# Moving the latent norm behind a whole projection job, and a weight split behind the key rotation, in a hand-scheduled transformer kernel

## The reference

```python
h = _rmsnorm(x, norm_g[l])
p = _split(h @ w_in[l])               # all projections of the layer
# branch A: latent attention
q  = _rmsnorm(cq, qa_g) @ w_uq        # cq: 256 features, its own norm
kv = _rmsnorm(ckv, kva_g) @ w_ukv     # ckv: 128 features, its own norm
k_rope = _rope(krope, cos, sin)       # a rotated key of 32 features
# branch C: sparse attention
score = relu(einsum('bqhd,bkd->bqhk', qidx, kidx))
index = einsum('bqh,bqhk->bqk', widx, score) * idx_scale
_, sel = lax.top_k(index, 128)        # 128 keys for each query
# branch B: differential attention; branch D: a gated short convolution
x = x + y @ w_out[l]
```

## Time and profile before

| what | value |
|---|---|
| median of 3 runs | 1886.48 us (1883.54 to 1887.06) |
| the profiled execution, its own time | 1886.48 us |
| span of the profiled execution | 1884.7 us |
| mean granted clock of PE | 0.992 |
| busy: PE | 1850.3 us, 98% |
| busy: PEld, DVE, ACT, POOL | 78%, 55%, 37%, 20% |
| chain that ended last, by engine | PE 93%, DVE 3%, issue 2%, ACT 1%, DMA 1% |

### The profile page before, as it was taken

The page is one execution under the profiler, slowest core; times in us unless marked ns, Lnnn a source line. Parts: engine busy times, 40 slices in busy tenths (PEclk is TensorE's granted clock), DMA queues, the critical chain, the costliest instruction groups (busy, mean ns, idle before and its releaser), DMA issues.

```text
span 1884.7 us, 26241 instructions
## 1 busy us (share of the span) xinstructions
PE 1850.3 (98%) x9284; PEld 1466.1 (78%) x9284; DVE 1038.5 (55%) x2106; ACT 691.8 (37%) x1274; POOL 386.1 (20%) x223
## 2 busy tenths in 40 slices
PE   6999999999999999999999999999999999999998
PEld 4767777876777788888888777778887888888887
DVE  5789777578977755554433333333644654454332
ACT  3444444335444432332233343333323423233222
POOL 2435253433534330000000222220110200000000
PEclk9999999999999999999999999999999999999999
DMA  5222112222211233222333412222221222232332
GB/s 190 76 82 68 57 56 81 91 68 79 77 58 53 84 123 95 100 94 95 101 107 105 140 56 68 81 77 79 90 90 45 79 90 90 100 100 90 105 107 89
DMA packets 48577, 165.65 MB, mean 88 GB/s; under 512 B 5592, under 2 KB 6104, under 8 KB 48472
## 3 DMA queue, kind: packets, MB, share of 16 engines
q1 hardware_dynamic: 47176, 161.88, 26.2%
q10 hardware_dynamic: 1296, 2.42, 0.4%
HBM read 162.12 MB, written 2.17 MB: 87 GB/s over the span
## 4 chain that ended last, share of the span: by engine, by line
PE 93%; DVE 3%; issue 2%; ACT 1%; DMA 1%; POOL 0%; POOLq 0%; DVEq 0%; SPq 0%; ACTq 0%
PE proj L863 75%; PE score L1081 3%; PE o L1117 2%; PE turned L1093 2%; PE proj L1236 2%; PE proj L1240 1%; PE turned L1304 1%; PE score L1298 1%; PE o L1328 1%; PE turned L833 1%; DVE wlo L1794 1%; PE o L1392 1%; PE score L1381 1%; ACT whi L1440 1%; PE proj L995 1%
## 5 line engine op out<-in xcount | busy, mean ns | idle before, releaser
L863 PE MATMUL proj<-hhi,whi 128*128 128x512 f32 x1488 | 600.2, 403 | 4.0 <-DVE wlo L1794 2.1
L863 PE MATMUL proj<-hlo,whi 128*128 128x512 f32 x1488 | 582.7, 392 | 0.0
L863 PE MATMUL proj<-hhi,wlo 128*128 128x512 f32 x1488 | 582.7, 392 | 0.0
L1440 ACT ACTIVATE whi<-ring 128x1024 fp32r<-128x1024 f32 x266 | 281.4, 1058 | 698.8 <-PE proj L863 652.8
L863 PEld LDWEIGHTS proj<-hhi,whi 128*128 128x128 f32 x1488 | 281.2, 189 | 97.6 <-issue 34.0
L863 PEld LDWEIGHTS proj<-hhi,wlo 128*128 128x128 f32 x1488 | 281.0, 189 | 60.8
L863 PEld LDWEIGHTS proj<-hlo,whi 128*128 128x128 f32 x1488 | 281.6, 189 | 55.9 <-issue 1.0
L1794 DVE TENSOR_TENSOR wlo<-ring,whi 128x1024 fp32r<-128x1024 f32 x187 | 228.5, 1222 | 158.8 <-ACT whi L1440 158.7
L655 POOL TENSOR_TENSOR wlo<-ring,whi 128x1024 fp32r<-128x1024 f32 x79 | 189.8, 2402 | 445.1 <-ACT whi L1440 445.0
L668 POOL TENSOR_TENSOR prob<-prob 128x512 f32<-128x512 f32 x30 | 46.3, 1544 | 854.6 <-ACT prob L1436 854.2
L1466 ACT ACTIVATE prob<-prob,negmax 128x256 f32<-128x256 f32 (+3 forms) x208 | 114.4, 551 | 136.0 <-DVE negmax L1838 136.0
(11 more groups left out here) (219 smaller groups left out, 2209.7 us busy)
## 6 DMA issues: line engine op xcount, KB each, us to landing
ring<-wstream SPq DMA_DIRECT2D x288, 512.0 KB, 3.5
arena<-lines SPq DMA_DIRECT2D x28, 256.0 KB, 5.5
arena<-x ACTq DMA_DIRECT2D x4, 512.0 KB, 6.2
out<-arena SPq DMA_DIRECT2D x8, 256.0 KB, 2.9
arena<-mem SPq DMA_DIRECT2D x1, 1024.0 KB, 9.4
par<-params ACTq DMA_DIRECT2D x3, 74.0 KB, 1.9
arena<-hot SPq DMA_DIRECT2D x2, 85.0 KB
arena<-rope SPq DMA_DIRECT2D x1, 128.0 KB, 6.0
```

Of the source, the lines that this page charges most:

```text
L863: mm = pe.matmul(b, rounded(w), rounded(rhs(v, k)), start=(first and n == 0 and p == 0), stop=(last and n == len(blocks) - 1 and p == 2))
L1440: act.activation(rounded(dst), src, ACT.Copy, scale=scale).then_inc(ready, 1)
```

## The change

- Sums of the latent squares: `LATENT_AT` goes from chunks 5 and 7 of BQ0 and 1 of BK0 to chunks 1, 3 and 5 of BK0.
- PE's wait for the diagonals and the 16 spreading matmuls go from behind chunk 0 of VT0 to behind the whole of VT0.
- DVE takes the means behind the eviction of BK0 instead of behind half 0 of the top-k; the diagonals come behind three small operations on `lam`, and no longer between half 2 and the eviction of BK0.
- `TOPK_EARLY` goes from 5 to 7: four halves (3 to 6) lie between the diagonals and the attention steps. They and the eviction of VT0 now stand ahead of the scaling of the latent tiles, not behind it.
- POOL takes the root behind the low part made after BK0 (the slot of BQ1), not ahead of it.
- POOL multiplies for the key rotation ahead of the low part made after KR (the slot of CQ1), not behind it, and ACT copies ahead of the high part of that slot.

```diff
-LATENT_AT = ((2, 5), (2, 7), (3, 1))
+LATENT_AT = ((3, 1), (3, 3), (3, 5))
...
-TOPK_FIRST, TOPK_EARLY = 3, 5
+TOPK_FIRST, TOPK_EARLY = 3, 7
...
 # POOL
                 prepare_after("KI")
-                prepare_after("KR")
-                after_low(SLOT_OF["CQ1"])
+                after_low(SLOT_OF["CQ0"])
                 pool.wait_ge(krope_moved, L + 1)
                 for n in range(2):
                     pool.tensor_tensor(krope[rows, n, :], krope[rows, n, :], ropes[rows, n, :], ALU.mult).then_inc(krope_step, 1)
                 pool.wait_ge(krope_step, L * 2 + 2)
+                prepare_after("KR")
                 prepare_after("CQ0")
-                for name in IDX_JOBS[:3]:
+                for name in IDX_JOBS:
                     prepare_after(name)
                 pool.wait_ge(mean_ready, L * 2 + 2)
                 root(2 * NT)
-                prepare_after(IDX_JOBS[3])
                 prepare_after("VT0")
...
 # PE
-                for k in range(KC):
-                    in_chunk("VT0", k)
-                    if k == 0:
-                        pe.wait_ge(spread_ready, L * LAYER_ROOTS + (R_LATENT + 1))
-                        spread_roots(turned[1], spread[0][:, 0:NT, :])
-                        spread_roots(turned[0], spread[0][:, NT:2 * NT, :]).then_inc(spread_done, 1)
+                in_job("VT0")
+                pe.wait_ge(spread_ready, L * LAYER_ROOTS + (R_LATENT + 1))
+                spread_roots(turned[1], spread[0][:, 0:NT, :])
+                spread_roots(turned[0], spread[0][:, NT:2 * NT, :]).then_inc(spread_done, 1)
...
 # ACT
-                prepare_after("KR")
                 wait_out(act, L, "KR")
                 act.activation(krope[HD:HD + 32, 1, :], krope[HD + 32:P, 1, :], ACT.Copy).then_inc(krope_moved, 1)
+                prepare_after("KR")
...
 # DVE
-                        topk_half(0)
-                        dve.wait_ge(latsum_done, L + 1)
-                        mean_squares(turned[0], ((0, 0, NT, 256), (NT, NT, NT, 128))).then_inc(mean_ready, 1)
-                        for n in range(1, TOPK_FIRST):
+                        for n in range(TOPK_FIRST):
                             topk_half(n)
-                        spread_diag(L * LAYER_ROOTS + R_LATENT, spread[0], range(2 * NT)).then_inc(spread_ready, 1)
                     out_of(name, *early[name])
 
+                dve.wait_ge(latsum_done, L + 1)
+                mean_squares(turned[0], ((0, 0, NT, 256), (NT, NT, NT, 128))).then_inc(mean_ready, 1)
                 dve.wait_ge(lam_exp, L + 1)
...
                 dve.tensor_tensor(lam[:, 5:6], lam[:, 4:5], par[:, P_LINIT:P_LINIT + 1], ALU.subtract).then_inc(lam_ready, 1)
+                spread_diag(L * LAYER_ROOTS + R_LATENT, spread[0], range(2 * NT)).then_inc(spread_ready, 1)
...
+                for n in range(TOPK_FIRST, TOPK_EARLY):
+                    topk_half(n)
+                stage_v(0)
                 dve.wait_ge(spread_done, L * 2 + 2)
                 for c in range(3):
                     t = cqn[:, c, :] if c < 2 else ckvn
                     dve.scalar_tensor_tensor(t, t, par[:, P_QA + c:P_QA + c + 1], turned[1 - c // 2][:, :], ALU.mult, ALU.mult)\
                         .then_inc(latent_ready, 1)
-                for n in range(TOPK_FIRST, TOPK_EARLY):
-                    topk_half(n)
-                stage_v(0)
```

## The result

| | before | changed |
|---|---|---|
| median, 4 runs each | 1886.43 us (1883.54 to 1887.06) | 1896.25 us (1894.1 to 1897.1) |
| span of the profiled execution | 1884.7 us | 1892.3 us |

The ratio is 1.0053 (95% interval 1.0036 to 1.007): 9.8 us slower by the medians, where 12.2 were forecast (1898.7, range 1892.5 to 1901). The direction and the three waits were right. Inside part B a wait that was forecast for both layers came in one, and the fall of PE's clock behind it was left out; the two errors have opposite signs.

The account below looks back on a forecast made before the run. PE bounds the kernel, 93% of the span, with about 3.1 us of idle to gain in both layers. 1.56 + 3.69 + 0.87 = 6.12 us a layer, 12.2 for both, on 1886.48 gives 1898.7 us, range 1892.5 to 1901.

Parts of the forecast that it names:

- the three waits: PE idles ahead of CQ1's first matmul (1.3 to 1.5 us), of spreading (about 4), of step 1's scores (0.8).
- part B: Root, diagonals and spreading: late root, and POOL's low part holding the eighth diagonal, delay step 0's scores 3.69 us a layer.
- The other side: Rival: the removed wait ahead of spreading was the costly one; at most 1.5 us gained for both layers, 1885.0; chance 0.02.
- Part A: Rotation ahead of the low part of CQ1's slot: POOL's low part comes late, PE's first CQ1 matmul loses 1.56 us a layer.
- the forecast case: Eighth diagonal held by POOL's low part in both layers, all three stalls paid: 12.2 us, range 1897 to 1900; chance 0.55.
- Part C: Scores of step 1: DVE's added work ahead makes the minima of step 0 late, PE waits 0.87 us a layer.
- What is late next: Minima of step 1 fit with 0.6 us to spare; by step 3 DVE is level again.
- The diagonals slip through: Rival: the diagonals pass ahead of POOL's low part; 3.7 us a layer, 7.5 for both, 1894.0; chance 0.28.
- DVE does not recover: Rival: step 2's 0.6 us slack is used up, another 2.4 us POOL operation waited out per layer; some 1903; chance 0.07.
- a hidden A: Rival that one stall is hidden: no CQ1 loss, diagonals free, 2.2 us a layer, 1890.9 or a little less; chance 0.08.
- a hidden C: Lower bound for the wait ahead of step 1's scores: 0 if PE is later than the minima after all.

Follow-up runs that it names:

- root_first: The changed kernel with POOL's root ahead of the low part behind BK0, as before the change; 1890.31 us, ratio 1.0031 to the kernel before.
- held: The changed kernel with the third operation on lam behind the wait for the root, so the diagonals start later; 1898.21 us, ratio 1.0072 to the kernel before.
- slip: The changed kernel with POOL also waiting for the diagonals before it starts the low part behind VT0; 1891.6 us, ratio 1.0038 to the kernel before.

## Why the prediction was right, and where not

- **What bounds the kernel.** Right: only PE's starts count, and the three new waits of PE make up the loss. The other side had no room, as all idle time of the two layers was 3.1 us.
- **Part A.** Forecast 1.56 us a layer. Right, 1.58 in both layers between matmul starts, of which PE's wait is 1.31; alone it made 1.0015, 2.8 us for both layers, by an interval of 1.1 to 4.5. The chain of it (copy at 56.46 to 57.09, multiplies, low part) is as worked out.
- **Part B, the step that failed first.** "The third `lam` operation falls under it, so it waits as the first did": it did not. It took 0.16 us at 97.46, with the root at 97.30 to 98.95, and so did one in root_first. A long row of POOL does not hold every two-operand DVE operation beside it: the low part did (2.37 us), the root did not. So the diagonals started 0.03 us behind the root, 5.37 us behind the first matmul of VT0 instead of the 5.52 worked out (97.1 less 91.58), and the margin at the eighth, which I had put at 0.15 to 0.2 us, was about zero. Held, where that operation is made to wait for the root, starts them 5.52 us behind (98.92 less 93.40), and both layers have the long wait. The case that I took for both layers came in one; the other had the rival's short wait, 1.45 us. Why the root held nothing is not shown.
- **Part B, what was left out.** The sum priced a wait as its length. In the held layer the granted clock fell behind it, and PE lost 1.4 us more in the spreading alone (3.48 against 2.05), so part B cost 5.01 instead of 3.69. As part C is hidden there, layer 0 lost 6.7 us instead of 6.1. One layer not held, the held one dearer: that adds to 10.5 us in the profile against 12.2 forecast. A small term was short too: from the first spreading matmul to the scores of step 0 it is 1.98 us in layer 1 (434.29 less 432.31), and the sum had 1.81. That the two large errors have opposite signs is luck; the forecast case itself, which is held, costs 13.6 by its ratio. That the range takes in the measured time is not luck, as its lower end was set by the rival.
- **Part C.** Forecast 0.87; PE's wait is 0.76 in layer 1, and 0.73 and 0.76 in slip. In layer 0 it isn't there, nor in either layer of held: the minima were to be 0.87 us too late, and the spreading at the lower clock brings PE to those scores 1.4 us later. So for a held layer the sum counts a wait that the slower matmuls cover, and leaves out these.
- **What is late next.** Right: in steps 2 and on the changed kernel has no wait of PE that the kernel before does not have; the later ones of the layer (0.45 and 0.20 us) are the same in both.
- **The rivals.** "The diagonals slip through", 1894.0, is the case of slip, 1891.6 us (by its ratio 7.2 us above the kernel before, where 7.5 were forecast). The truth lies between the likeliest case and this rival, one layer each. "DVE does not recover" did not occur, nor did "the other side", nor a hidden A; a hidden C did, in the held layer.

## What to carry to other kernels

Before a step is put behind others on a queue, list every engine on the path from it to the waiting one, and lay their rows on one time axis: here a root of 1.65 us moved behind one low part cost its wait, and put eight diagonals in the way of the next low part. Where two requests for something that excludes each other come within the error of the sum, price both outcomes, each layer for itself; a wait of the engine that may go first (as in slip) can be the faster schedule. Price a long idle stretch of PE (here 3.65 us) with the slow matmuls behind it, and ask what other wait these slow matmuls then cover.

## What the runs showed of the hardware

- Behind the idle stretches of PE of 3.65 to 3.77 us at this place the granted clock was 0.50 to 0.59 in the windows read (the changed kernel, held), and behind the waits of 1.45 us the 16 spreading matmuls kept their 2.05 us. The fall adds 1.3 to 1.7 us in the spreading matmuls (3.38 us in the second profile of the changed kernel to 3.78 in held, instead of 2.05).
- A POOL subtraction of 128 x 1024 held a DVE operation on one column for 2.37 us, while a POOL power on 128 x 8, shown as 1.65 us, did not hold the one-column operations beside it (0.16 us at 97.46 in the changed kernel, at 94.67 in root_first).
- A POOL subtraction of that size got in between two diagonals of a running row of eight: the eighth shows 2.46 us instead of 0.28 (changed kernel, layer 0).
- POOL's low part 1.42 us behind the first diagonal came ahead of the eighth, and 1.43 us behind it after the eighth, in two profiles alike.
